# Mamba-2 state-space heads on one core: where the low parts are made, in which order the first output slot multiplies, and which engine squares

## The reference, cut to what matters

```python
def mamba2_mixer(h, w_in, conv_w, conv_b, dt_bias, a_log, d_skip, norm_w, w_out):
    ...
    y = ssd_chunked_scan(xs, dt.reshape(bsz, L, G, R), a.reshape(G, R), ...)
    y = y + d_skip.reshape(G, R)[..., None] * xs
    y = y.reshape(bsz, L, SSM_D_INNER)
    y = rmsnorm(y * jax.nn.silu(z), norm_w)
    return y @ w_out

# in the scan, for the single chunk of 256 tokens and a state of zeros:
        decay = jnp.exp(jnp.where(causal, seg, -jnp.inf))
        cb = jnp.einsum('btgn,bsgn->btsg', c_k, b_k)
        w = cb[..., None] * decay * dt_k[:, None]
        y_intra = jnp.einsum('btsgr,bsgrp->btgrp', w, x_k)
```

## Time and profile before

| what | us |
|---|---|
| median of three runs (lowest, highest) | 1845.71 (1842.48, 1847.34) |
| the profiled execution | 1848.24 |
| its span | 1846.4 |
| TensorE busy in the span | 1789.1 |
| VectorE busy | 1315.2 |
| ScalarE busy | 985.6 |
| POOL busy | 436.6 |

### The profile page before, as it was taken

The page is one execution under the profiler, slowest core; times in us unless marked ns, Lnnn a source line. Parts: engine busy times, 40 slices in busy tenths (PEclk is TensorE's granted clock), DMA queues, the critical chain, the costliest instruction groups (busy, mean ns, idle before and its releaser), DMA issues.

```text
span 1846.4 us, 36129 instructions
## 1 busy us (share of the span) xinstructions
PE 1789.1 (97%) x14414; PEld 1720.4 (93%) x14414; DVE 1315.2 (71%) x1782; ACT 985.6 (53%) x1440; POOL 436.6 (24%) x444
## 2 busy tenths in 40 slices
PE   4999999999999999999999999999999999999998
PEld 3999999979999999999979999979999989689998
DVE  6787877888777577768876545787666767866665
ACT  3555565474645465446465445666454533765453
POOL 1222200051222122221144211383222100432221
PEclk9999999999999999999999999999999999999999
DMA  9877734835577647674924545423555443035551
GB/s 400 323 274 297 292 126 171 291 141 221 202 284 267 258 181 296 252 275 179 373 87 180 182 182 183 159 69 116 183 186 189 171 158 135 26 115 177 187 182 69
DMA packets 51205, 371.11 MB, mean 201 GB/s; under 512 B 5680, under 2 KB 5808, under 8 KB 6192
## 3 DMA queue, kind: packets, MB, share of 16 engines
q1 hardware_dynamic: 41904, 302.85, 44.7%
q0 software_dynamic: 9216, 67.11, 9.6%
HBM read 368.89 MB, written 1.05 MB: 200 GB/s over the span
## 4 chain that ended last, share of the span: by engine, by line
PE 82%; DVE 7%; ACT 4%; issue 3%; POOL 2%; DMA 1%; SPq 0%; POOLq 0%; DVEq 0%; ACTq 0%
PE gu L766 39%; PE acc L774 8%; PE acc L773 8%; PE acc L775 8%; PE gu L1128 2%; PE gu L1268 2%; PE gu L773 2%; PE gu L775 2%; PE gu L774 2%; DVE w_lo L1986 2%; DVE mring L2001 1%; DVE arena L2289 1%; ACT w_hi L1516 1%; PE acc L1339 1%; PE acc L1240 1%
## 5 line engine op out<-in xcount | busy, mean ns | idle before, releaser
L1986 DVE TENSOR_TENSOR w_lo<-ring,w_hi 128x2048 fp32r<-128x2048 f32 x263 | 606.1, 2308 | 259.6 <-ACT w_hi L1516 259.6
L1516 ACT ACTIVATE w_hi<-ring 128x2048 fp32r<-128x2048 f32 x263 | 501.3, 1908 | 63.7 <-PE acc L775 49.4
L766 PE MATMUL gu<-Hs_hi,w_hi 128*128 128x258 f32 (+1 forms) x2080 | 419.7, 283 | 0.2 <-DVE Hs_lo L2059 0.2
L766 PE MATMUL gu<-Hs_lo,w_hi 128*128 128x258 f32 (+1 forms) x2080 | 416.2, 282 | 0.0
L766 PE MATMUL gu<-Hs_hi,w_lo 128*128 128x258 f32 (+1 forms) x2080 | 415.7, 281 | 0.0
L687 POOL TENSOR_TENSOR arena<-arena,rstd 128x512 f32<-128x512 f32 x132 | 209.3, 1586 | 814.8 <-ACT arena L1550 776.7
L766 PEld LDWEIGHTS gu<-Hs_hi,w_hi 128*128 128x128 f32 x2080 | 320.2, 189 | 1.2 <-DVE Hs_lo L2059 0.4
L766 PEld LDWEIGHTS gu<-Hs_hi,w_lo 128*128 128x128 f32 x2080 | 320.3, 189 | 0.0
L766 PEld LDWEIGHTS gu<-Hs_lo,w_hi 128*128 128x128 f32 x2080 | 320.0, 189 | 0.0
L774 PE MATMUL acc<-hid_lo,w_hi 128*128 128x256 f32 x1056 | 297.8, 282 | 0.0
L773 PE MATMUL acc<-hid_hi,w_hi 128*128 128x256 f32 x1056 | 296.4, 281 | 0.8 <-DVE hid_lo L2218 0.8
(11 more groups left out here) (418 smaller groups left out, 2923.7 us busy)
## 6 DMA issues: line engine op xcount, KB each, us to landing
ring<-in_weights SPq DMA_DIRECT2D x276, 1024.0 KB, 4.8
mring<-in_mods POOLq DMA_DIRECT2D x64, 1024.0 KB, 6.4
mring<-in_mods SPq DMA_DIRECT2D x8, 1024.0 KB, 9.4
con<-in_constants SPq DMA_DIRECT2D x1, 1344.0 KB, 14.6
X<-in_x SPq DMA_DIRECT2D x1, 1024.0 KB, 12.3
out<-X SPq DMA_DIRECT2D x1, 1024.0 KB, 3.9
cact<-in_c SPq DMA_DIRECT2D x1, 512.0 KB, 3.6
vec<-in_vectors SPq DMA_DIRECT2D x1, 498.0 KB, 6.4
```

What stands on the lines that cost most here:

```text
L766: ins = mm(dst, part, x_lo if i == 1 else x_hi, start=start and i == 0, stop=stop and i == 2, skip_group_check=True)
L1516: act.activation(w_hi[buffer_of(n0, s)][:, :], ring[:, n % RING, :], ACT.Copy).then_inc(hi_ready, 1)
L1986: dve.tensor_tensor(w_lo[b][:, :], ring[:, n % RING, :], w_hi[b][:, :].bitcast(F32), ALU.subtract).then_inc(split_ready, 1)
```

## The change

- POOL: still multiplies tiles 0 to 11 with the gate, but squares only the even ones; it adds the square of tile m - 1 behind the product (and square) of tile m.
- ScalarE: squares the odd tiles below 12 too, each right behind its high part; tiles 12 to 15 as before.
- VectorE: makes low parts only at odd steps from j = 9 on, tile (j - 9) / 2. That is tiles 0 to 4 in the loop; `LOW_Z` = 5, so the eleven low parts of tiles 5 to 15 stand behind the loop.
- TensorE, slot 24 (m = 0): first high by high and low weights by high for all 16 tiles (it waits for `zhi_ready`), then the 16 products with low parts (it waits for `h_ready`). The number of matmuls stays 48.

```diff
--- before.py
+++ after.py
@@ -238,6 +238,7 @@
         Wd = part(at + 2 * INNER, WBUF, 2, TRI)
         assert at + 2 * INNER + WBUF * 2 * TRI <= SPLIT_AT[0]
         YBUF = 4
+        LOW_Z = (KI + 2 - 9 + 1) // 2
         POOL_Z = 12
         Yt = H[:, 0:YBUF, :]
         sqz = H[:, YBUF:KD, :]
@@ -634,18 +635,27 @@
                 pool.tensor_copy(id_bf[:, :], ident)
                 pool.tensor_copy(mask_bf[:, :], cs("mask_sq", 0, P)).then_inc(sel_ready, 1)
                 load_mods(2 * MSLOTS + MRING, 2 * MSLOTS + 8 + MRING)
-                for m in range(KI):
-                    square = sqz[:, 0 if m == 0 else 1 + m % 2, :]
+
+                def square_of(m):
+
+                    return sqz[:, 0 if m == 0 else 1 + m % 2, :]
+
+                for m in range(KI + 1):
                     if m < POOL_Z:
                         pool.wait_ge(y_free, m + 1)
                         pool.tensor_tensor(Z[:, m, :], Z[:, m, :], Yt[:, m % YBUF, :], ALU.mult).then_inc(zg_ready, 1)
-                        pool.wait_ge(zg_ready, m + 1)
-                        pool.tensor_tensor(square, Z[:, m, :], Z[:, m, :], ALU.mult).then_inc(sqz_ready, 1)
-                    if m:
-                        pool.wait_ge(sqz_ready, m + 1)
-                        if m >= 2:
-                            pool.wait_ge(sqz_added, m - 1)
-                        pool.tensor_tensor(sqz[:, 0, :], sqz[:, 0, :], square, ALU.add).then_inc(sqz_added, 1)
+                        if m % 2 == 0:
+                            pool.wait_ge(zg_ready, m + 1)
+                            if m:
+                                pool.wait_ge(sqz_ready, m)
+                            if m >= 3:
+                                pool.wait_ge(sqz_added, m - 2)
+                            pool.tensor_tensor(square_of(m), Z[:, m, :], Z[:, m, :], ALU.mult).then_inc(sqz_ready, 1)
+                    if m >= 2:
+                        pool.wait_ge(sqz_ready, m)
+                        if m >= 3:
+                            pool.wait_ge(sqz_added, m - 2)
+                        pool.tensor_tensor(sqz[:, 0, :], sqz[:, 0, :], square_of(m - 1), ALU.add).then_inc(sqz_added, 1)
 
             def bare_add(sq0, square, done):
 
@@ -1002,12 +1012,22 @@
                 for m in range(KD):
                     state["split"] += 1
                     pe.wait_ge(split_ready, state["split"])
-                    for k in range(KI):
-                        if m == 0:
+                    if m == 0:
+                        hi, lo = (w[buffer_of(n0, 24)] for w in (w_hi, w_lo))
+                        for k in range(KI):
+                            pe.wait_ge(zhi_ready, k + 1)
+                            for i, w in enumerate((hi, lo)):
+                                mm(acc_t(0), w[:, k * P:(k + 1) * P], Z_hi[:, k, :], start=(k == 0 and i == 0), stop=False,
+                                   skip_group_check=True)
+                        for k in range(KI):
                             state["h"] += 1
                             pe.wait_ge(h_ready, state["h"])
-                        ins = three(acc_t(m), buffer_of(n0, 24 + m), slice(k * P, (k + 1) * P), Z_hi[:, k, :],
-                                    Z_lo[:, k, :], start=(k == 0 and m % 2 == 0), stop=(k == KI - 1))
+                            ins = mm(acc_t(0), hi[:, k * P:(k + 1) * P], Z_lo[:, k, :], start=False, stop=(k == KI - 1),
+                                     skip_group_check=True)
+                    else:
+                        for k in range(KI):
+                            ins = three(acc_t(m), buffer_of(n0, 24 + m), slice(k * P, (k + 1) * P), Z_hi[:, k, :],
+                                        Z_lo[:, k, :], start=(k == 0 and m % 2 == 0), stop=(k == KI - 1))
                     ins.then_inc(slot_done, 1)
                     if m == 0:
                         pe.wait_ge(sqz_added, KI - 1)
@@ -1634,9 +1654,10 @@
                 def high_z(m):
                     act.wait_ge(zg_ready, m + 1)
                     act.activation(Z_hi[:, m, :], Z[:, m, :], ACT.Copy, scale=v1("ssm_norm", m)).then_inc(zhi_ready, 1)
-                    if m >= POOL_Z:
+                    if m >= POOL_Z or m % 2:
                         act.wait_ge(sqz_ready, m)
-                        act.wait_ge(sqz_added, m - 2)
+                        if m >= 3:
+                            act.wait_ge(sqz_added, m - 2)
                         act.activation(sqz[:, 1 + m % 2, :], Z[:, m, :], ACT.Square).then_inc(sqz_ready, 1)
 
                 act.wait_ge(misc_used, 3)
@@ -2351,9 +2372,9 @@
                         weights(j)
                     if j >= 2:
                         skip(j - 2)
-                    if j >= 5:
-                        low_z(j - 5)
-                for m in range(KI - 3, KI):
+                    if j >= 9 and j % 2:
+                        low_z((j - 9) // 2)
+                for m in range(LOW_Z, KI):
                     low_z(m)
                 low(n0, 25)
                 low(n0, 26)
```

## The result

| kernel | median us (lowest to highest, runs) |
|---|---|
| before | 1845.07 (1842.48 to 1848.62, 12) |
| after | 1848.49 (1846.06 to 1849.85, 12) |

The ratio after to before is 1.0016 with a 95% interval of 1.0009 to 1.0023, which is +3.0 us (1.7 to 4.2). The kernel became slower by less than the 0.3% that the prediction called no change, and by more than the +1.6 us it forecast. The profiled execution took 1849.85 us.

What follows compares the result with a forecast made beforehand. TensorE paces the heads; before m=1, its chain and VectorE's end within 0.06 us. VectorE's later end +0.7 and the clock +0.9 gave +1.6 us: 1847.3 us on the median, range 1844.4 to 1850.4.

Steps and rivals of the forecast that it cites:

- rival C: In the heads, ScalarE and POOL wait for each other, delaying the exponentials: +6.0 us, 1851.7 us; chance 0.05.
- its cover: In the heads, some 4 us before VectorE's skip, four tiles later, needs the POOL product delayed by waiting for ScalarE's square.
- y(15): TensorE's product of pair 15, behind the heads; forecast to start at 415.50, 1.43 us earlier, as POOL no longer falls behind.
- the old gap: TensorE's 2.35 us wait ahead of the product of pair 15 before the change; half clock behind it cost 1.65 us, hidden.
- the lower of the two starts: Slot m=0 was forecast to start at 416.4 (full clock) to 417.0 (half clock) instead of 418.40.
- m=1 is set by VectorE's low parts: Behind the heads, late low parts make m=1 wait for VectorE, paying back the 1.43 us: +0.7 us, bounds -0.6 and +1.6.
- The sum without meetings: VectorE's new order added up behind the last exponentials: twelve low parts to 422.50, weights' low part to 424.79, before 425.41.
- Meetings with POOL: VectorE instructions slowed by POOL's additions 11 to 15 behind the heads: three of five at 0.45 us each, 1.35 us.
- Rival B: Each VectorE meeting costs a whole POOL instruction, 3.65 instead of 1.35 us; with a full clock fall +4.7, 1850.4 us; chance 0.08.
- The clock: Half clock behind TensorE's new gap ahead of m=1, where nothing hides it: 0.9 us taken, between 0 and 1.65.
- The upper bound of 2.75 us: Largest clock cost behind the new gap, from a 5.5 us half-clock stretch at the stage's start.
- the three signs of being wrong: m=1 starting before 424.5, four steps of the heads over 8.7 us, or TensorE waiting for a high part in m=0.

Runs made afterwards that it cites:

- a: Changed kernel with VectorE's low parts back in the loop over the heads, one a step from step 5, three behind it; ratio to before 0.9996.
- e: Changed kernel with one low part a step from step 9 on, so seven stand behind the loop instead of eleven; ratio to before 1.0020.
- b: Changed kernel with TensorE's old tile-by-tile order in slot m=0, low parts still late and squares on ScalarE; ratio to before 1.0011.
- the fill: Changed kernel with products of zeros in TensorE's idle time, ahead of the last ten low products of m=0 and behind the norm's sums; ratios 1.0016 and 1.0015.
- d: Kernel before with only the odd tiles' squares moved to ScalarE and POOL's addition one tile later; ratio to before 0.9996.
- fill_again: Second run of the changed kernel with TensorE's idle time ahead of m=1 filled by products of zeros; ratio to before 1.0015.
- c_fill: First run of the changed kernel with TensorE's idle time ahead of m=1 filled by products of zeros; ratio to before 1.0016.
- h_halves: Changed kernel with low parts back in the loop and the low part of slot 25's weights made in two halves; ratio to before 0.9993.
- halves_again: Second run of the changed kernel with low parts in the loop and slot 25's weights' low part in two halves; ratio to before 1.0004.

## Why the prediction was right or wrong, point by point

- **TensorE paces the heads, no wait for ScalarE or POOL (right).** 8.57 us for four steps, and rival C did not occur. POOL's wait for the square, 0.68 us, stayed under its cover.
- **y(15) earlier by 1.43 us (nearly right).** Measured 1.19 from y(14), or 1.43 against the last exponentials, since y(14) came 0.24 earlier itself. The half clock behind the old gap did not come again there, and m=0 took the lower of the two starts.
- **m=1 is set by VectorE's low parts (right).** The prediction's "seven more" are those behind step 15; behind the loop it is eight, eleven instead of three. The sum without meetings was exact in its steps: skip(13) at 414.88 forecast and 411.85 + 3.03 = 414.88 measured, product 13 at 415.38 and 415.39. Experiments a and e tie the start of the weights' low part to the number of late low parts, and b shows that the order of slot m=0 doesn't move m=1.
- **Meetings with POOL, 1.35 us taken (too small).** VectorE came to the weights at 421.24 + 3.03 = 424.27 and not at 422.50: 1.77 us. The rows are the low part of 0.95 us at 412.70, the product of 0.65 us at 414.08 and two of the twelve low parts (POOL's two additions from 415.66 to 417.47). On before's clock of the trace m=1 starts at 423.57 + 3.03 = 426.60: late by 1.13 us where 0.7 was forecast. Rival B's whole POOL instruction per meeting (0.73 us) is above what the rows show, 0.5 us.
- **The clock, 0.9 us taken (the step that failed in size).** Slot m=1 took 8.06 and 7.83 us instead of 5.83. The forecast let half of a low stretch fall into the gap. In fact the stretch at half clock was 6.7 us long, not 3.3. Ahead of it the last 16 products of slot m=0, waiting for their low parts, stood spread over 4.38 us instead of 1.9, which the forecast had not counted as light work; with the old order (b, one profile) the fall came ahead of m=1 and took nothing from it. By the windows the stretch ran from about 421.8, ahead of the gap, to 428.5, 4.93 us into the slot. The upper bound of 2.75 us, from the start of the stage, was the better row.
- **The sum.** +0.7 + 0.9 = +1.6 forecast; +1.13 + 2.23 = +3.4 at this place in the profile; +3.0 (1.7 to 4.2) timed. As no timed gain of the fill is shown, the agreement of the last two numbers may be partly luck. The 5.5 us that the prediction took for what a measurement can tell from no change was too much: twelve runs of each kernel gave +3.0 with 1.3 us to each side.
- **What the profile would show.** On before's clock of the trace, y(15) is at 415.50 as forecast, the weights' high part was ready some 3 us ahead of VectorE, no product with a high part waited in m=0, and none of the three signs of being wrong came. Narrowly missed: a gap of 1.16 us ahead of y(15) (none over 1 forecast), the row of low parts ending at 424.34 (422.5 to 424), an idle TensorE for 1.34 us ahead of m=1 (1.5 or more), released at 426.60 (425 to 426.5).
- **What stays open.** Whether the fall of the clock costs its 2 us in the timed runs as well, and why e is at 1.0020. In the profiles the stretches at half clock elsewhere, in code that no edit touches, differ by more than that (the section on the hardware, below), so the timings can't settle it.

## What to carry to other kernels

When two engines' chains end together at one instruction, shortening one gives nothing, and paying for it with the other is a loss: fill the idle time of the paced loop with the engine that is late behind it, not the other way round. To test that, put products of zeros in the gap of the engine that waits: if the next stage starts at the same time, the gap was hidden. Where a stage needs only half of a converted tile to start, convert it in halves; and count the clock as a price of any light stretch or gap that is moved to where nothing hides it: in the profiles here it made slot m=1 longer by 1.5 to 2.2 us in four executions (the changed kernel twice, d and e) and by nothing in the others.

## What the runs showed of the hardware

The granted clock fell and rose at other places, too, in code that is the same in all kernels. Stretches of TensorE alone (busy, granted clock, DMA share, GB/s) in the kernel before and in fill_again:

```profile
220.00:236.00 16.00, 12.58 (x75) 0.68 0.35 127
260.00:272.00 12.00, 9.92 (x72) 0.86 0.46 171
...
1208.00:1224.00 16.00, 14.06 (x58) 0.89 0.39 132
1236.00:1252.00 16.00, 13.71 (x70) 0.89 0.00 1
```

```profile
220.00:236.00 16.00, 12.34 (x84) 0.79 0.23 75
260.00:272.00 12.00, 9.92 (x82) 1.00 0.35 121
...
1208.00:1224.00 16.00, 14.09 (x66) 1.00 0.37 132
1236.00:1252.00 16.00, 11.19 (x65) 1.00 0.01 2
```

Time at half clock is (1 - granted) x 2 x the stretch: 10.2, 3.4, 3.5 and 3.5 us in these four of before, 6.7, 0, 0 and 0 in fill_again. Half of the difference of 13.9 us is 7 us of TensorE work, more than any effect studied here. Not all of it reaches the end of the kernel. At 1216 us the conformer's sums wait for POOL and VectorE:

```profile
PE gu L1203 <- DVE arena L2565: 0.7, 1, 0.7
```

```profile
PE gu L1223 <- DVE arena L2586: 2.0, 1, 2.0
```

The kernel before, slow at 1216 to 1224, waited there 0.7 us, the changed one, at the full clock, 2.0: 1.3 us of the stretch was hidden. Two executions of one kernel show the scatter directly. With the fill (c_fill, fill_again) y(14) begins at 413.20 and 409.03, and from the spread to the end it is 1417.4 and 1415.0 us; with the halves (h_halves, halves_again) it is 411.72 and 410.88, and 1414.8 and 1417.7 us. This is why a difference of 2 us in one profile between equal code says nothing, and why the distances from y(14) to slot m=1, which agree within 0.01 us between two executions of one kernel (13.13 and 13.12, 9.59 and 9.59), say more than the whole time. The end of slot m=1 is less steady where the clock falls (21.19 and 20.95).

A second thing: a low part on VectorE (two SBUF inputs) that met a POOL addition took 0.95 us instead of 0.48 (at 412.70 in the changed kernel), a product that met only the end of one 0.65 instead of 0.42 (414.08), and two POOL additions in such company 0.9 us each instead of 0.73 (415.66). Each side paid, and VectorE the most.
